# Where VectorE does the conformer's convolution steps of the first token half: one block behind the second value convolution, or spread between the token mixes

## The chip, the cores and the metric

One core of a Trainium2 chip runs the whole program. The time is the device time of one execution in microseconds (us); of several executions the median is given. TensorE (PE in the profile) multiplies matrices into PSUM, VectorE (DVE) and ScalarE (ACT) work on PSUM and SBUF, GpSimd (POOL) on SBUF, SyncE (SP) issues the copies from HBM.

## The reference, cut to what matters

Two transformer blocks follow each other. The first begins with four token mixers side by side (gMLP, gated delta rule, RWKV-7, a conformer convolution), each on 256 channels of 1024 tokens. Two pieces of it meet in this change:

```python
def conformer_conv(z, conv_w, conv_b, ln_g, ln_b):          # CONF_CONV = 31 taps
    z1, z2 = jnp.split(z, 2, axis=-1)
    h = z1 * jax.nn.sigmoid(z2)
    h = causal_depthwise_conv(h, conv_w) + conv_b
    h = layer_norm(h, ln_g, ln_b, LN_EPS)
    return jax.nn.silu(h)

# in rwkv7_time_mix
    P_prev = jnp.pad(P, ((0, 0), (1, 0), (0, 0)))[:, :-1]
    P = P + (P_prev - P) * mu
```

## The kernel before, in words

Channels lie on the 128 partitions and tokens along the free dimension. The first mixers work through the tokens in two halves of 512 (h = 0 and 1); 256 channels are two tiles (i = 0 and 1) of 128 x 512. Each engine runs a hand-written list of calls, strictly in order, and waits on semaphores where it needs another engine.

TensorE's list is made of units (L407): a unit multiplies 256 columns of w_in with the normalised tokens of one half, 32 matmuls into two PSUM tiles, and carries the name of what it makes (k, v, q, cs, cz, dg, r, rk, rv, rx, gu, gv). Between them stand the small products: transposes (L449), Gram matrices (L508), the block solves (L543 to L617) and so on. The weights of a unit are fetched by SyncE into one of two slots, as soon as TensorE has ended the unit two before (L795).

PSUM has 8 banks, and `Tiles.open` hands them out in turn: the n-th tile opened takes bank n modulo 8, and TensorE waits there until the engine that read the tile eight before has "taken" it. In the stretch that matters the tiles opened are, in order, gx 0, gx 1 (made for `spread_out`, L1500), then tok v 0, v 1, kk 0, kk 1, a 0, a 1 (taken by ScalarE, L1057 to L1061), then tok k 0 and k 1, which need the banks of gx 0 and gx 1, and after those the Gram tiles LT, AK, RB, RK (L508), which need the banks of v, kk, a and k.

On VectorE:

- `glu(0)` multiplies the two parts of the conformer's input. `taps_of(0)` is a generator of 62 steps, 31 taps by two channel tiles. Each step but the first two is one instruction (L1480) that multiplies the shifted 128 x 512 input by a weight per channel and adds it to the output; a step needs the step two before it, that of the same tile. `some(taps, n)` issues the next n steps.
- `mix(name, j, h)` (L1281, L1284) finishes a token mix behind ScalarE's L946, which first scales the unit's PSUM tile; one such pair for each tile i.
- `dn_scalars`, `values`, `q_scale`, `dn_decays` (L1295 to L1334) are small steps of the delta rule; `dn_grams` (L1342) masks its Gram tiles, beside GpSimd's L1674; `inverse` (L1369 to L1395) inverts triangular blocks.
- `conv("v", 1)` (L1254, L1269) is the short convolution of the second half's values; `spread_out(0)` (L1500, L1506) takes gx 0 and gx 1; `rw_grams(0)` (L1351 to L1357) masks RWKV's Gram tiles.

The result of the 62 steps is first read in `layer("cf", 0)`, far behind this stretch, and GpSimd copies the last 30 input columns of the half into the margin of the next when all 62 are done (L1703).

Of the kernel before, what the change touches and what calls it, by code (L numbers as in the profile page):

```python
# [30 lines left out]
class Env:  # L31
# [8 lines left out]
    def col(self, name, k=0):  # L40
        j = self.cols_at[name] + k
        return self.cols[:, j:j + 1]
# [271 lines left out]
def mixers_of_first_block(env):  # L314
# [21 lines left out]
    lt, rb, rk = (by_chunk(env.words(t, 0, 2 * T)) for t in (24, 26, 28))  # L336
# [43 lines left out]
    with stage(env, *names) as (block, *sems):  # L380
# [847 lines left out]
        def _(dve):  # L1228
# [46 lines left out]
            def mix(name, j, h, tiles_of=range(2)):  # L1275
                for i in tiles_of:
                    n = 2 * j + i
                    m, mu = rw[("r", "k", "v", "xwag")[j]][i], col("rw_mu", n)
                    dve.wait_ge(s["m_ready"], 8 * h + n + 1)
                    ps = tiles.ps(name, h, i)  # L1280
                    ins = v.scalar_tensor_tensor(m[:, 1:], ps[:, 0:HALF - 1], mu, m[:, 1:], ALU.mult, ALU.add)  # L1281
                    if h == 0:
                        ins.then_inc(s["mixed"], 1)
                        tiles.take(v.tensor_copy(hist_rw[:, n:n + 1], ps[:, HALF - 1:HALF]), name, h, i)  # L1284
                    else:
                        tiles.take(ins, name, h, i)
                        v.scalar_tensor_tensor(m[:, 0:1], hist_rw[:, n:n + 1], mu, m[:, 0:1], ALU.mult, ALU.add
                                               ).then_inc(s["mixed"], 1)
# [4 lines left out]
            def dn_scalars(h):  # L1293
                tiles.wait_taken(dve, "abt", h)
                dn_step(h, 1, v.tensor_tensor(chunks8(small["y"]), chunks8(small["ab"]), cols_of("dn_sgn", 8).unsqueeze(1).broadcast_to([P, CHUNKS, 8]), ALU.mult))  # L1295
                dn_step(h, 2, v.tensor_tensor(small["y"], small["y"], cols_of("dn_off", 32), ALU.add))
                if h == 0:
                    dve.wait_ge(s["rate_ready"], 1)
                dve.wait_ge(s["dn_act"], 8 * h + 3)
                dn_step(h, 3, v.scalar_tensor_tensor(small["sp"], small["y"], 0.0, small["l"], ALU.max, ALU.add))  # L1300
                sp = small["sp"].rearrange("p (c m) -> p c m", m=8)
                dn_step(h, 4, v.scalar_tensor_tensor(per_head(small["a16"]), sp[:, :, HEADS:8], -1.0, per_head(small["rate"]),
                                                     ALU.mult, ALU.mult))
                for j in range(2):
                    tiles.wait_taken(dve, "kt", h, j)
                sqk = env.words(O0, 0, 2 * T).rearrange("p (k two t) -> p k two t", k=2, two=2)[:, :, h, :]
                dn_step(h, 5, v.tensor_tensor(sqk, two(env.tile(4)), two(env.tile(4)), ALU.mult))
                dn_step(h, 6, v.tensor_reduce(small["ssq"].rearrange("p (k e) -> p k e", k=2),
                                              sqk.rearrange("p k (e d) -> p k e d", d=HD), AX_X, ALU.add))
                dve.wait_ge(s["dn_act"], 8 * h + 4)  # L1310
                dn_step(h, 7, v.scalar_tensor_tensor(per_head(small["lnc"]), sp[:, :, 0:HEADS], -1.0, per_head(small["lnq"]),
                                                     ALU.mult, ALU.subtract))

            def values(h):
                dve.wait_ge(s["dn_act"], 8 * h + 5)
                for j in range(2):
                    tiles.wait_taken(dve, "vt", h, j)
                x = env.words(2, 0, 2 * T).rearrange("p (n d) -> p n d", d=P)[:, :, 0:HD]
                v.tensor_tensor(x, x, small["vsc"].unsqueeze(2).broadcast_to([P, 16, HD]), ALU.mult).then_inc(s["r_values"], 1)

            def q_scale(h):
                for i in range(2):
                    dve.wait_ge(s["qn_ready"], 2 * h + i + 1)
                    v.scalar_tensor_tensor(q[i], q[i], HD ** -0.5, temp_g[1][i], ALU.mult, ALU.mult).then_inc(s["q_ready"], 1)

            def dn_decays(h):
                tiles.wait_taken(dve, "g", h)
                g, last = small["gsb"][:, 0:16], small["gsb"][:, 16:32]
                dn_step(h, 8, v.tensor_tensor(small["bias"], small["lnc"], g, ALU.subtract))
                dn_step(h, 9, v.tensor_tensor(small["kx"], small["bias"], last, ALU.add))  # L1330
                for e in range(2):
                    rows = slice(e * HD, (e + 1) * HD)
                    src = last[rows].rearrange("p (c i e) -> p c i e", i=2, e=2)[:, :, :, e]
                    dn_step(h, 10 + e, v.tensor_copy(small["dec2"][rows].rearrange("p (c i) -> p c i", i=2), src))  # L1334

            def dn_grams(h):
                for j in (0, 2):
                    for name, dst in (("KK", lt), ("QK", rb)):
                        for g in (j, j + 1):
                            dve.wait_ge(s["decay_step"], 8 * h + 4 + g + 1)  # L1340
                            tiles.wait(dve, name, h, g)
                            tiles.take(v.tensor_tensor(part(dst, g), quad(tiles.ps(name, h, g)), quad(exps[g % 2]), ALU.mult), name, h, g)  # L1342
# [127 lines left out]
            def taps_of(h):  # L1470
                w = lambda tap, i: col("cf_conv_w", 2 * tap + i)
                for back in range(TAPS_CF):
                    for i in range(2):
                        o, x = out_half(6 + i, h), cfh[:, i, TAPS_CF - 1 - back:TAPS_CF - 1 - back + HALF]
                        if back == 0:
                            dve.wait_ge(s["glu_ready"], 2 * h + i + 1)
                            ins = v.tensor_scalar(o, x, w(TAPS_CF - 1, i), col("cf_conv_b", i), ALU.mult, ALU.add)
                        else:
                            dve.wait_ge(s["cf_step"], 62 * h + 2 * back + i - 1)
                            ins = v.scalar_tensor_tensor(o, x, w(TAPS_CF - 1 - back, i), o, ALU.mult, ALU.add)  # L1480
                        ins.then_inc(s["cf_step"], 1)
                        yield

            def some(taps, n):
                for _ in range(n):
                    next(taps, None)
# [9 lines left out]
            def spread_out(h):  # L1496
                for i in range(2):
                    t = gm_v[i].rearrange("p (c t) -> p c t", t=P)
                    tiles.wait(dve, "gx", h, i)
                    ins = v.tensor_tensor(t, by_chunk(tiles.ps("gx", h, i)), b_s[:, i, :].unsqueeze(1).broadcast_to([P, CHUNKS, P]),  # L1500
                                          ALU.add)
                    tiles.take(ins, "gx", h, i)
                for i in range(2):
                    tiles.wait_taken(dve, "gx", h, i)
                    tiles.wait_taken(dve, "gu", h, i)
                    v.tensor_tensor(out_half(i, h), out_half(i, h), gm_v[i], ALU.mult)  # L1506
# [59 lines left out]
            conv("q", 0)  # L1566
            glu(0)
            taps = taps_of(0)
            some(taps, 12)
            dn_scalars(0)  # L1570
            mix("r", 0, 0)
            values(0)
            q_scale(0)
            some(taps, 4)
            mix("rk", 1, 0)
            dn_decays(0)
            some(taps, 6)
            mix("rv", 2, 0)
            some(taps, 14)
            mix("rx", 3, 0)  # L1580
            some(taps, 2)
            dn_grams(0)
            some(inverse("dn", 0), BLOCK)
            layer("gm", 0)
# [6 lines left out]
            dn_final(0)  # L1591
            decayed(0)
            conv("v", 1)
            some(taps, 62)
            spread_out(0)
            rw_grams(0)
            steps = inverse("rw", 0)
# [8 lines left out]
            taps = taps_of(1)  # L1606
# [3646 lines left out]
```

## Time and profile before

| | |
|---|---|
| median of 3 runs | 3183.69 us (3182.38 to 3184.23) |
| the profiled execution's own time | 3183.69 us |
| its span, from the first to the last instruction | 3181.4 us |
| busy share of the span | PE 97%, DVE 62%, POOL 42%, ACT 27% |

The profile shows for every instruction when it began and how long it took. A pause is printed in square brackets in front of the instruction that ended it, with its length and the instruction that released it. PEclk is the share of TensorE's full clock that was granted: 1.00 is 2.4 GHz, 0.50 is 1.2 GHz.

### The profile page before, as it was taken

Reading aid. Unit: us, or ns where it says so; the run is one execution under the profiler, and the core shown is the slowest. Engines: PE = TensorE matmul, PEld = TensorE weight load, DVE = VectorE, ACT = ScalarE, POOL = GpSimd, SP = SyncE. Lnnn points to the kernel's source line nnn. Section 1 sums busy time; section 2 is a strip of 40 time slices with the busy share of each in tenths; the row PEclk is TensorE's granted clock in tenths of the full one; section 3 lists DMA queues with packets and bytes.
Section 4 is the critical chain, followed back from the end, with each engine's and each line's share of the span. In section 5 each row is a group of like instructions: output and inputs, shape, how many; then the busy total and the mean of one; then the engine's idle time right before and its main releaser. Section 6 shows DMA issues by size and latency. Waiting matters only on the chain.

```text
span 3181.4 us, 35229 instructions
## 1 busy us (share of the span) xinstructions
PE 3073.9 (97%) x13146; PEld 2078.0 (65%) x13146; DVE 1984.8 (62%) x2716; ACT 861.0 (27%) x1530; POOL 1345.7 (42%) x1016
## 2 busy tenths in 40 slices
PE   8998998999999999999999999999999999999997
PEld 3445563874578888788644544544555588888886
DVE  2386888653578788787526654753125665577876
ACT  3343334321233333100213335203223344410002
POOL 0010010002599999555411000351015798855555
PEclk9999999999999999999999999999999999999998
DMA  4211111152222222666212111212121233376652
GB/s 142 67 60 34 50 34 53 54 172 93 80 80 85 85 100 90 226 234 227 67 54 90 57 54 53 77 43 66 53 80 53 113 140 146 126 254 234 220 197 81
DMA packets 206279, 335.70 MB, mean 106 GB/s; under 512 B 10145, under 2 KB 123297, under 8 KB 205345
## 3 DMA queue, kind: packets, MB, share of 16 engines
q1 hardware_dynamic: 204688, 330.45, 29.9%
q10 hardware_dynamic: 1424, 3.02, 0.3%
q8 instruction: 107, 1.75, 0.2%
q14 instruction: 60, 0.48, 0.0%
HBM read 269.21 MB, written 64.23 MB: 105 GB/s over the span
## 4 chain that ended last, share of the span: by engine, by line
PE 82%; DVE 9%; POOL 4%; ACT 2%; issue 1%; DMA 1%; ACTq 0%; SPq 0%; DVEq 0%; POOLq 0%
PE psum L3627 21%; PE psum L3907 14%; PE psum L181 10%; PE psum L2680 8%; PE psum L407 7%; PE psum L2082 3%; PE psum L4474 3%; PE psum L3644 2%; PE psum L563 1%; DVE arena L1380 1%; DVE arena L1378 1%; PE psum L4451 1%; PE psum L4412 1%; PE psum L2088 1%; DVE arena L1480 1%
## 5 line engine op out<-in xcount | busy, mean ns | idle before, releaser
L3627 PE MATMUL psum<-arena 128*128 128x256 f32 x2632 | 598.0, 381 | 14.2 <-DVE arena L3672 7.4
L3907 PE MATMUL psum<-arena 128*128 128x256 f32 x2660 | 585.9, 383 | 10.2 <-POOL arena L3933 5.3
L3907 PEld LDWEIGHTS psum<-arena 128*128 128x128 f32 x2660 | 510.7, 192 | 84.0 <-POOL arena L3933 7.1
L3627 PEld LDWEIGHTS psum<-arena 128*128 128x128 f32 x2632 | 499.4, 191 | 93.6 <-DVE arena L3672 11.2
L407 PE MATMUL psum<-arena 128*128 128x512 f32 x768 | 337.6, 598 | 7.1 <-DVE arena L1236 4.9
L181 PE MATMUL psum<-arena 128*128 128x512 f32 x768 | 332.4, 592 | 1.5 <-ACT arena L4644 1.5
L407 PEld LDWEIGHTS psum<-arena 128*128 128x128 f32 x768 | 146.0, 192 | 189.5 <-issue 184.8
L181 PEld LDWEIGHTS psum<-arena 128*128 128x128 f32 x768 | 145.8, 190 | 182.1 <-issue 180.6
L2680 PE MATMUL psum<-arena 128*128 128x512 f32 x576 | 251.5, 595 | 0.0
L2680 PEld LDWEIGHTS psum<-arena 128*128 128x128 f32 x576 | 109.0, 191 | 136.4 <-issue 136.4
L2369 DVE TENSOR_TENSOR arena<-arena 128x1024 f32<-128x1024 f32 x77 | 144.3, 1874 | 33.6 <-ACT arena L3664 23.8
L3930 POOL TENSOR_TENSOR arena<-arena 128x512 f32<-128x512 f32 (+1 forms) x49 | 74.9, 1529 | 208.6 <-PE psum L3907 78.6
L3627 PE MATMUL psum<-arena,consts_sb 128*128 128x256 f32 x632 | 155.7, 379 | 3.7 <-POOL consts_sb L3719 3.2
L3504 POOL TENSOR_TENSOR arena<-small_sb,consts_sb 128x512 f32<-128x512 f32 x16 | 16.2, 1041 | 324.3 <-PE psum L2760 169.5
L4871 DVE TENSOR_TENSOR arena<-arena 128x1024 f32<-128x1024 f32 x88 | 145.5, 1653 | 12.8 <-ACT arena L3655 8.3
L3664 ACT ACTIVATE conformer<-psum 128x256 f32<-128x256 f32 x238 | 90.6, 382 | 200.6 <-PE psum L3627 196.6
L4991 POOL TENSOR_TENSOR arena<-arena 128x512 f32<-128x512 f32 x75 | 98.5, 1314 | 102.4 <-DVE arena L4748 71.1
L2518 POOL TENSOR_TENSOR arena<-arena 128x512 f32<-128x512 f32 x42 | 57.4, 1366 | 181.0 <-ACT arena L2215 180.0
L3627 PEld LDWEIGHTS psum<-arena,consts_sb 128*128 128x128 f32 x632 | 119.7, 190 | 20.8 <-POOL consts_sb L3719 3.6
L3672 DVE TENSOR_TENSOR arena<-psum,conformer 128x256 f32<-128x256 f32 x238 | 98.6, 417 | 51.0 <-PE psum L3627 46.8
L2082 PE MATMUL psum<-arena 128*128 128x512 f32 x256 | 112.5, 592 | 0.0
L4474 PE MATMUL psum<-arena 128*128 128x512 f32 x224 | 97.0, 593 | 0.9 <-DVEq L241 0.9
(540 smaller groups left out, 4830.7 us busy)
## 6 DMA issues: line engine op xcount, KB each, us to landing
arena<-w_in SPq DMA_DIRECT2D x42, 1024.0 KB, 5.3
arena<-mlp_w SPq DMA_DIRECT2D x72, 512.0 KB, 6.9
arena<-w_ffn_down SPq DMA_DIRECT2D x36, 512.0 KB, 6.8
arena<-mlp_w SPq DMA_DIRECT2D x8, 2048.0 KB, 8.6
mlp_hidden_T<-arena SPq DMA_DIRECT2D x32, 512.0 KB, 2.6
arena<-mlp_hidden_T SPq DMA_DIRECT2D x16, 1024.0 KB, 5.6
arena<-w_out SPq DMA_DIRECT2D x12, 1024.0 KB, 5.4
mlp_hidden_B<-arena SPq DMA_DIRECT2D x24, 512.0 KB, 2.6
```

The source lines that it names most:

```text
L181: mm = nc.tensor.matmul(self.out(i, x.shape[1]), part, x, start=(kk == 0), stop=(kk == self.kt - 1))
L407: mm = nc.tensor.matmul(ps, slot(u)[:, k, m * P:(m + 1) * P], hn(k, h), start=(k == 0), stop=(k == KD - 1))
L2082: mm = nc.tensor.matmul(ps, plain_raw(v)[:, k, m * P:(m + 1) * P], half_of(env, N0, k, h), start=(k == 0), stop=(k == KD - 1))
L2369: hidden.mark(v_.tensor_tensor(to, one, two, ALU.add), name, q)
L2680: mm = nc.tensor.matmul(ps, slot(n)[:, k, m * P:(m + 1) * P], x_half(k, h), start=(k == 0), stop=(k == KD - 1))
L3627: mm = self.env.nc.tensor.matmul(self.ps(n, m), left[:, k, :], right[:, k, :], start=(m in (1, 5, 2) and k == 0), stop=(k == 1), skip_grou ...
L3664: self.copied.mark(self.env.nc.scalar.activation(to, self.ps(n, m), ACT.Copy), name, n)
L3672: self.blocks.mark(self.env.nc.vector.tensor_tensor(self.to(n, i, j), self.ps(n, m), self.temps[t][n % 2], ALU.add), name, n)
L3907: mm = self.env.nc.tensor.matmul(ps[:, 256 * r:256 * r + 256], left[:, s, r * P:(r + 1) * P], right[:, s, :], start=(first and s == 0 and ...
L4474: mm = nc.tensor.matmul(ps, left, mix_right[m](k), start=(k == 0), stop=(k == 3))
L4871: blocks.mark(v_.tensor_tensor(to, one, two, op), name, q)
L4991: fin(pool, nc.gpsimd.tensor_tensor(dst, dst, src, ALU.add), sem, value)
```

## The change

Before, the 62 steps of the first half were issued as 12, 4, 6, 14 and 2 between the calls in front of `dn_grams(0)`, and the other 24 in one block behind `conv("v", 1)`. After, all 62 are issued in front of the last mix, as 25, 3, 3, 4, 8, 11 and 8. For that, three calls of `mix` are split into one call for each channel tile, with steps between the two. No instruction is added, removed or altered; only VectorE's list has another order.

```diff
             taps = taps_of(0)
-            some(taps, 12)
+            some(taps, 25)
             dn_scalars(0)
-            mix("r", 0, 0)
+            mix("r", 0, 0, (0,))
+            some(taps, 3)
+            mix("r", 0, 0, (1,))
             values(0)
+            some(taps, 3)
             q_scale(0)
             some(taps, 4)
-            mix("rk", 1, 0)
+            mix("rk", 1, 0, (0,))
+            some(taps, 8)
+            mix("rk", 1, 0, (1,))
             dn_decays(0)
-            some(taps, 6)
-            mix("rv", 2, 0)
-            some(taps, 14)
+            some(taps, 11)
+            mix("rv", 2, 0, (0,))
+            some(taps, 8)
+            mix("rv", 2, 0, (1,))
             mix("rx", 3, 0)
-            some(taps, 2)
             dn_grams(0)
...
             conv("v", 1)
-            some(taps, 62)
             spread_out(0)
             rw_grams(0)
```

## Rows read from the trace of the kernel before

**Rows 1.** Page: share of the chain that ended last, by engine.
```profile
PE 82%; DVE 9%; POOL 4%; ACT 2%; issue 1%; DMA 1%; ACTq 0%; SPq 0%; DVEq 0%; POOLq 0%
```

**Rows 2.** Chain that ended last, 296 to 345 us: start, duration, what.
```profile
303.61 14.65 DVE arena L1480 x23
...
319.50 0.61 DVE arena L1500
...
320.25 1.94 PE psum L449 x8
```

**Rows 3.** Timeline of PE, 300 to 335 us: start, duration, instructions merged, pause before.
```profile
300.02 3.02 PE L449 MATMUL psum<-consts_sb,arena 128*128 128x128 f32 x24
320.25 1.94 PE L449 MATMUL psum<-consts_sb,arena 128*128 128x128 f32 x8 [17.22 <-DVE arena L1500]
322.13 4.63 PE L508 MATMUL psum<-arena 64*128 64x128 f32 x64
...
328.62 3.84 PE L508 MATMUL psum<-arena 64*128 64x128 f32 x64
...
334.23 13.95 PE L407 MATMUL psum<-arena 128*128 128x512 f32 x32
```

**Rows 4.** Timeline of DVE, 303 to 321 us.
```profile
303.52 15.98 DVE L1480 SCALAR_TENSOR_TENSOR arena<-conformer,cols_sb,arena 128x512 f32<-128x512 f32 x24
319.43 1.28 DVE L1500 TENSOR_TENSOR arena<-psum,arena 128x512 f32<-128x512 f32 x2
```

**Rows 5.** Windows: busy by engine, then PEclk, DMA share, GB/s.
```profile
303.00:320.00 17.00, 0.04 (x1) 0.00 (x0) 16.93 (x28) 4.18 (x8) 0.23 (x1) 0.61 0.01 2
320.00:323.00 3.00, 2.75 (x16) 2.45 (x18) 1.91 (x4) 1.19 (x2) 0.00 (x0) 0.50 0.00 0
...
348.00:396.00 48.00, 47.70 (x155) 23.45 (x155) 41.65 (x86) 17.68 (x30) 0.00 (x0) 1.00 0.24 70
```

**Rows 6.** Timeline of DVE, 98 to 179 us.
```profile
115.70 0.19 DVE L1295 TENSOR_TENSOR small_sb<-small_sb,cols_sb 128x32 f32<-128x32 f32 x1 [9.65 <-ACT small_sb L875]
...
129.19 0.75 DVE L1281 SCALAR_TENSOR_TENSOR arena<-psum,cols_sb,arena 128x511 f32<-128x511 f32 x1 [3.01 <-ACT arena L946]
...
134.69 1.29 DVE L1324 SCALAR_TENSOR_TENSOR arena<-arena 128x512 f32<-128x512 f32 x2 [3.19 <-ACT arena L928]
...
145.52 0.75 DVE L1281 SCALAR_TENSOR_TENSOR arena<-psum,cols_sb,arena 128x511 f32<-128x511 f32 x1 [6.05 <-ACT arena L946]
...
154.83 0.75 DVE L1281 SCALAR_TENSOR_TENSOR arena<-psum,cols_sb,arena 128x511 f32<-128x511 f32 x1 [3.71 <-ACT arena L946]
...
161.70 0.75 DVE L1281 SCALAR_TENSOR_TENSOR arena<-psum,cols_sb,arena 128x511 f32<-128x511 f32 x1 [6.05 <-ACT arena L946]
...
162.43 9.36 DVE L1480 SCALAR_TENSOR_TENSOR arena<-conformer,cols_sb,arena 128x512 f32<-128x512 f32 x14
...
175.43 0.75 DVE L1281 SCALAR_TENSOR_TENSOR arena<-psum,cols_sb,arena 128x511 f32<-128x511 f32 x1 [2.92 <-ACT arena L946]
...
176.16 2.44 DVE L1480 SCALAR_TENSOR_TENSOR arena<-conformer,cols_sb,arena 128x512 f32<-128x512 f32 x2
178.53 0.68 DVE L1342 TENSOR_TENSOR arena<-psum,arena 128x512 f32<-128x512 f32 x1
```

**Rows 7.** Timeline of POOL, 116 to 180 us: all its work there.
```profile
120.18 5.08 POOL L1668 TENSOR_TENSOR arena<-small_sb,consts_sb 128x512 f32<-128x512 f32 x4 [62.92 <-DVE small_sb L1302]
176.79 2.95 POOL L1674 TENSOR_TENSOR arena<-arena,consts_sb 128x512 f32<-128x512 f32 x2 [51.53 <-ACT arena L973]
```

**Rows 8.** Timeline of ACT, 306 us: the last copies before the pause.
```profile
306.08 1.11 ACT L1059 ACTIVATE arena<-psum 128x512 f32<-128x512 f32 x2
```

**Rows 9.** Timeline of PE: units (32 matmuls) behind two shorter pauses.
```profile
503.48 15.70 PE L407 MATMUL psum<-arena 128*128 128x512 f32 x32 [2.18 <-DVE arena L1281]
...
2282.74 13.97 PE L4451 MATMUL psum<-arena 128*128 128x512 f32 x32 [1.21 <-ACT arena L4665]
```

**Rows 10.** Page, DMA issues: count, KB each, us to landing.
```profile
arena<-w_in SPq DMA_DIRECT2D x42, 1024.0 KB, 5.3
```

## The prediction

> **What bounds the kernel now.** I read the page first. The chain that ended last lies on TensorE for 82% of the span and on VectorE for 9% [rows 1], so VectorE work is worth something only where it is in that chain. The change moves instructions of L1480, so next I asked the chain for the stretch behind `conv("v", 1)`. The steps stand in it: 23 of them in one piece from 303.61, then L1500, then TensorE's L449 at 320.25 [rows 2]. Then I read the two engines there. TensorE ends the transposes of v, kk and a at 300.02 + 3.02 = 303.04, and then pauses 17.22 us until VectorE's L1500 releases it [rows 3]. VectorE meanwhile does 24 steps in 15.98 us, from 303.52, and starts L1500 at 319.43 [rows 4]. The reader should see why the one waits for the other. The tiles of tok k need the banks of gx, gx is taken by `spread_out`, and `spread_out` stands behind the 24 steps, which nothing needs yet. This is an order in a list, not a lack of VectorE time.
>
> The windows add something that the chain does not say. TensorE's mean clock in the 17 us of the pause is 0.61, and in the 3 us behind it 0.50, which is 1.2 GHz [rows 5]. So the pause is paid twice: once as idle time and once as slow matmuls behind it.
>
> Last I looked at where the steps go. Between 98 and 179 us VectorE has seven pauses that matter: 9.65, 3.01, 3.19, 6.05, 3.71, 6.05 and 2.92 us, 34.6 us together, each ended by ScalarE [rows 6].
>
> **What the change removes.** The 24 steps leave the path: L1500 can start at 303.52 instead of 319.43 [rows 4], which is 15.91 us. What it needs is there: gx was made by matmuls in front of the transposes that TensorE started at 300.02 [rows 3].
>
> The second part is the clock. After the change TensorE pauses from 303.04 until L1500 has taken gx 0. Before, it went on 0.82 us after L1500 had started (320.25 against 319.43), so now that is at 303.52 + 0.82 = 304.34: a pause of 1.3 us. No row shows this very pause, so I bound its effect from both sides. If the clock falls nevertheless, as behind the pause of 2.18 us, whose unit took 15.70 us [rows 9] against the 13.95 of an undisturbed one [rows 3], nothing more is gained. If it stays up, the eight L449 take a third of the 3.02 us of the 24 before them, 1.01 instead of 1.94, and the 64 L508 the 3.84 of their second group instead of 4.63 [rows 3]: 0.93 + 0.79 = 1.72 us. A unit behind a pause of 1.21 us took 13.97 [rows 9], as an undisturbed one; 1.3 is nearest to that row, so I take the clock as kept.
>
> Not all of the 1.72 can be had, because other engines then set the pace. The second tile of tok k must wait for the second L1500 (half of 1.28 us later). And ScalarE, whose list is in order, ends its copies of kk and a at 306.08 + 1.11 = 307.19 [rows 8]. It can take tok k only then, two copies of the same size, until about 308.3, and the tiles of RK need those two banks. RK is the last quarter of the 64 L508, some 0.96 us, so it ends at about 309.4. With a cold clock it would end at 322.13 + 4.63 - 15.91 = 310.85. That is 1.4 us; I take 1.3 for the semaphores between.
>
> Sum: 15.9 + 1.3 = 17.2 us.
>
> **What it adds in front.** The 24 steps now lie in the pauses. One step costs 9.36 / 14 = 0.67 us [rows 6], and 15.98 / 24 gives the same [rows 4]. The first pause begins at 115.70 - 9.65 = 106.05; 13 more steps are 8.7 us against 9.65. Then 3 are 2.0 against 3.01, 3 are 2.0 against 3.19, and 8 are 5.3 against 6.05. Before the first rv mix 5 more are 3.3 against 3.71, and before the second 8 are 5.3 against 6.05 [rows 6]. Every group fits, with 0.35 us to spare at the tightest. So each mix and each small step starts when it did, and ScalarE and TensorE see no difference; cost 0. The four steps in front of the rk mix stay where they were. The cover is thin, but if a group runs over, the mixes behind it only come late, and the list has slack again: the last 2.92 us pause stays, and 14 + 2 steps that stood around the rx mix are gone, 9.36 + 2.44 us [rows 6].
>
> The two steps that go from 176.16 took 2.44 us, 1.22 each, beside GpSimd's L1674 [rows 6, 7]. The first Gram mask there could start 178.53 - 176.16 = 2.4 us sooner, but the one behind it waits for GpSimd, and TensorE has no use for it: I count nothing. In the new places GpSimd is idle except from 120.18 to 125.26 [rows 7], when VectorE does `dn_scalars` as before. GpSimd's margin copy waits for step 62 and comes sooner; it is 0.23 us of the window in which it stands [rows 5] and nothing waits closely for it. No copy from HBM is issued by what moves.
>
> **What is late next.** Behind 304 TensorE has no pause to give the gain back in: from 348 to 396 it is busy 47.70 of 48 us, VectorE 41.65 [rows 5], and both start from the L508 that have moved. The weights move along, since a unit's copy is issued when the unit two before has ended. A copy lands in 5.3 us [rows 10] and has a whole unit, 13.95 us [rows 3], to do so.
>
> So the span is 3181.4 - 17.2 = 3164.2 us. The profiled execution took 3183.69 us, 2.3 around its span, and equals the median of the runs; so the forecast is 3183.69 - 17.2 = 3166.5 us.
>
> **The rivals.**
>
> First, the clock falls all the same. For it speaks that 2.18 us were enough once [rows 9], and that TensorE will have small waits behind the 1.3 us pause too, at the second gx and at tok k. Then only the 15.9 us come: 3167.8 us. The Trainium skill, "TensorE: Matmul & The Clock Gate", section "A second HAM failure mode: psum-queue depth-cycling", says that a PE that idles briefly again and again while it goes round the PSUM banks can swing between the two clock levels. By that rule this rival would be the likelier one; the unit behind 1.21 us at full speed [rows 9] speaks against it, and no row here has several short waits in the same few us. I give it 0.24.
>
> Second, the steps do not fit, and the change only moves the delay. If none of the pauses could be used (each pause's releaser then comes as much later), 24 x 0.67 = 16.0 us would arrive at `dn_grams` and from there at TensorE: 17.2 - 16.0 = 1.2 us faster, 3182.5. Against it: the pauses end with ScalarE, which waits for TensorE's units and not for VectorE, so they are real. 0.03.
>
> Third, the gain is given back at a wait that does not move, say a unit whose weights come late. The price is at most 17.2 us, so the time lies up to 3183.7; it begins where a copy takes longer than the 13.95 us of a unit, against 5.3 [rows 3, 10]. 0.03.
>
> Fourth, the other side: the steps are slower in the new places, as the two beside GpSimd. The 62 steps have the time that 38 took before, 36 x 0.67 + 2.44 = 26.4 us, and the 34.6 us of pauses, 61.0 together. With 17.2 us of gain on top they may take 78.2, 1.26 each, before the kernel is slower; at 1.40 each they take 86.8, which makes 8.6 us more, 3192.3. Even the pace beside GpSimd, 1.22, stays below, and GpSimd works in only 5.08 of these 78 us [rows 7]. The Trainium skill, "GPSIMD Engine Reference", section "8. Key points", says that GpSimd shares its SBUF interfaces with VectorE and that instructions with two SBUF inputs, which these steps are, contend with it. No run here shows which other engine could do the same. 0.02.
>
> **How the numbers follow.** The forecast holds 0.68, the rivals 0.24, 0.03, 0.03 and 0.02. The predicted time is the forecast's, 3166.5. The clock's bounds give 3183.7 - 15.9 - 1.7 = 3166.1 to 3167.8. The three runs lie 1.3 below and 0.5 above their median, which makes 3164.8 to 3168.3. A later short pause, like that of 2.18 us, can lose or keep its clock when what comes before has moved: 15.70 - 13.95 = 1.75 us, taken as 1.8 upwards and 1.0 downwards. So the range is 3163.8 to 3170.1. 0.2%, 6.4 us, is about what a measurement of this kernel can tell from no change. Faster by more holds the forecast, the first rival and half of the third, 0.68 + 0.24 + 0.015, about 0.94; within it the second and the rest of the third, 0.04; slower the fourth, 0.02.
>
> **What would show it.** In the profile after: no L1480 between 300 and 320 us; L1500 at about 303.5; TensorE's pause in front of the last eight L449 about 1.3 us instead of 17.2; PEclk 1.00 from 304 to 310; the unit that starts at 334.23 now at about 317.0; the pauses of rows 6 down to 0.3 to 1.2 us with the instructions behind them at the same times. The prediction is wrong if a mix or `dn_scalars` starts later than before by more than a few tenths, if TensorE shows a pause between 98 and 300 us that it did not have, or if the difference of 17 us at that unit is smaller at 400 us or at the end.

## The result, and the profile after

The changed kernel takes 3166.89 us in the median of six runs (3163.02 to 3169.91), the kernel before 3183.96 (3182.38 to 3184.63): a ratio of 0.9946, 95% interval 0.9936 to 0.9957, so 0.54% faster. The forecast was 3166.5 us in a range of 3163.8 to 3170.1.

I read the profile after in the order of the forecast's own list. First the timeline of PE in the stretch behind `conv("v", 1)`, which answers to [rows 3]:

```profile
299.59 3.02 PE L449 MATMUL psum<-consts_sb,arena 128*128 128x128 f32 x24
303.92 1.16 PE L449 MATMUL psum<-consts_sb,arena 128*128 128x128 f32 x8 [1.32 <-DVE arena L1500]
305.01 4.03 PE L508 MATMUL psum<-arena 64*128 64x128 f32 x64
...
310.91 3.84 PE L508 MATMUL psum<-arena 64*128 64x128 f32 x64
...
316.51 13.95 PE L407 MATMUL psum<-arena 128*128 128x512 f32 x32
```

The pause in front of the last eight L449 is 1.32 us instead of 17.22. All of this profile lies 0.43 us earlier than that of before (the 24 L449 at 299.59, not 300.02). The difference is there from the first unit on (19.25 us against 19.68), far in front of anything that the change touches, so here and below I measure from the start of those 24 to the start of the next unit, L407: 334.23 - 300.02 = 34.21 us before, 316.51 - 299.59 = 16.92 after. That is 17.29 us less.

On DVE, [rows 4] become one line. The steps are gone, and L1500 follows the last instructions of `conv("v", 1)` directly:

```profile
301.81 1.37 DVE L1269 SCALAR_TENSOR_TENSOR arena<-small_sb,cols_sb,arena 128x1 f32<-128x1 f32 x6
303.09 1.28 DVE L1500 TENSOR_TENSOR arena<-psum,arena 128x512 f32<-128x512 f32 x2
```

The windows, which answer to [rows 5]. PEclk is the third number from the right:

```profile
303.00:306.00 3.00, 2.08 (x24) 1.82 (x26) 2.58 (x5) 2.98 (x7) 0.00 (x0) 1.00 0.00 0
306.00:310.00 4.00, 4.00 (x61) 3.88 (x58) 2.90 (x5) 2.72 (x6) 0.00 (x0) 1.00 0.00 0
...
331.00:379.00 48.00, 47.66 (x157) 23.25 (x155) 41.71 (x85) 17.86 (x30) 0.00 (x0) 1.00 0.25 76
```

TensorE's clock stays at 1.00 through the pause and behind it, where it was 0.61 and 0.50. In the 48 us behind the next unit, from 331 to 379 us (348 to 396 before), TensorE is as busy as before, 47.66 of 48 us.

In front, the timeline of DVE that answers to [rows 6]:

```profile
115.27 0.19 DVE L1295 TENSOR_TENSOR small_sb<-small_sb,cols_sb 128x32 f32<-128x32 f32 x1 [1.04 <-ACT small_sb L875]
...
128.76 0.75 DVE L1281 SCALAR_TENSOR_TENSOR arena<-psum,cols_sb,arena 128x511 f32<-128x511 f32 x1 [1.02 <-ACT arena L946]
...
134.26 1.29 DVE L1324 SCALAR_TENSOR_TENSOR arena<-arena 128x512 f32<-128x512 f32 x2 [1.21 <-ACT arena L928]
...
145.09 0.75 DVE L1281 SCALAR_TENSOR_TENSOR arena<-psum,cols_sb,arena 128x511 f32<-128x511 f32 x1 [0.76 <-ACT arena L946]
...
154.40 0.75 DVE L1281 SCALAR_TENSOR_TENSOR arena<-psum,cols_sb,arena 128x511 f32<-128x511 f32 x1 [0.39 <-ACT arena L946]
...
161.26 0.75 DVE L1281 SCALAR_TENSOR_TENSOR arena<-psum,cols_sb,arena 128x511 f32<-128x511 f32 x1 [0.75 <-ACT arena L946]
...
175.00 0.75 DVE L1281 SCALAR_TENSOR_TENSOR arena<-psum,cols_sb,arena 128x511 f32<-128x511 f32 x1 [6.05 <-ACT arena L946]
...
177.67 0.69 DVE L1342 TENSOR_TENSOR arena<-psum,arena 128x512 f32<-128x512 f32 x1 [1.85 <-POOL arena L1678]
```

The pauses have shrunk to 1.04, 1.02, 1.21, 0.76, 0.39 and 0.75 us, and the instruction behind each starts where it did, less the 0.43 us of the whole profile (115.27 for 115.70, 161.26 for 161.70). Nothing is late.

The first block solve of RWKV starts 17.7 us sooner than before (L543, 392.60 for 410.27), and the span is 18.1 us shorter: 0.43 in front of the change, 17.29 in the stretch, the remaining 0.4 in later stages. Only the 17.29 us are shown to come from the change.

### The profile page after: what moved, and what is told of

Its sections match the earlier page's. It is cut to its first block, busy times and chain, and to the rows that moved or that the text cites. A ratio compares the mean times of both kernels' runs of the same rounds, so it can differ in the third digit from the quotient of the medians.

```text
span 3163.3 us, 35229 instructions
## 1 busy us (share of the span) xinstructions
PE 3067.8 (97%) x13146; PEld 2073.4 (66%) x13146; DVE 1983.9 (63%) x2716; ACT 862.1 (27%) x1530; POOL 1345.1 (43%) x1016
## 3 DMA queue, kind: packets, MB, share of 16 engines
q8 instruction: 107, 1.75, 0.2%
## 4 chain that ended last, share of the span: by engine, by line
PE 82%; DVE 9%; POOL 4%; ACT 2%; issue 1%; DMA 1%; ACTq 0%; SPq 0%; DVEq 0%; POOLq 0%
PE psum L3631 21%; PE psum L3911 13%; PE psum L181 10%; PE psum L2684 8%; PE psum L407 7%; PE psum L2086 3%; PE psum L4478 3%; PE psum L3648 2%; PE psum L563 1%; DVE arena L1380 1%; DVE arena L1378 1%; PE psum L4455 1%; PE psum L4416 1%; PE psum L2092 1%; DVE arena L1391 1%
## 5 line engine op out<-in xcount | busy, mean ns | idle before, releaser
L407 PE MATMUL psum<-arena 128*128 128x512 f32 x768 | 337.6, 598 | 7.2 <-DVE arena L1236 4.9
L407 PEld LDWEIGHTS psum<-arena 128*128 128x128 f32 x768 | 146.0, 192 | 189.5 <-issue 184.7
L4875 DVE TENSOR_TENSOR arena<-arena 128x1024 f32<-128x1024 f32 x88 | 149.0, 1693 | 12.6 <-ACT arena L3659 8.1
```

Source lines behind the costliest of these rows:

```text
L407: mm = nc.tensor.matmul(ps, slot(u)[:, k, m * P:(m + 1) * P], hn(k, h), start=(k == 0), stop=(k == KD - 1))
L4875: blocks.mark(v_.tensor_tensor(to, one, two, op), name, q)
```

## The experiments

Times are medians; the kernel before ran on the same chip beside each group: 3184.39 us beside lump_late, lump_early, warm and behind_grams, 3183.54 beside keep3, keep8, second_half and after_again, 3185.12 beside warm16 and all_first. "Stretch" is the measure of above, from the 24 L449 to the next unit. In kernels with added or removed lines the line numbers behind them are shifted by up to 5.

| run | us | ratio to before, interval | TensorE's pause before L449 | stretch |
|---|---|---|---|---|
| after_again | 3166.95 | 0.9947, 0.9930 to 0.9963 | 1.32 | 16.92 |
| lump_early | 3166.48 | 0.9944, 0.9929 to 0.9959 | 1.32 | 16.91 |
| all_first | 3174.11 | 0.9967, 0.9954 to 0.9980 | 1.32 | 16.92 |
| lump_late | 3186.70 | 1.0007, 0.9998 to 1.0017 | 1.32 | 16.92 |
| behind_grams | 3184.04 | 0.9999, 0.9990 to 1.0009 | 1.32 | 16.92 |
| keep3 | 3170.19 | 0.9955, 0.9941 to 0.9970 | 3.30 | 20.22 |
| keep8 | 3174.32 | 0.9969, 0.9957 to 0.9981 | 6.62 | 23.80 |
| warm16 | 3183.61 | 0.9998, 0.9989 to 1.0008 | filled | 32.63 |
| warm | 3194.24 | 1.0031, 1.0018 to 1.0044 | filled | 44.70 |
| second_half | 3155.91 | 0.9912, 0.9897 to 0.9927 | 1.31 | 16.92 |

**Is the spreading needed, and how deep is the cover?** Three kernels are the one before with the 24 steps in another place (in all_first all 62 steps, so 50 are moved), and with no mix split.

```diff
# lump_early: in front of dn_scalars(0)
-            some(taps, 12)
+            some(taps, 36)
             dn_scalars(0)
...
-            some(taps, 62)
             spread_out(0)
```

> Before, with the 24 steps put in one block in front of dn_scalars(0) (36 instead of 12), no mix split. They run over ScalarE's release there (9.65 us of pause for 16 us of steps), so dn_scalars starts some 6.4 us later. Theory (TensorE needs those small results only about 20 us later, and VectorE catches up in its later pauses): the time of the change, 3165 to 3169, the same 1.3 us pause before L1500, no new pause of TensorE between 98 and 300. Rival (the spreading itself is needed): a new TensorE pause between 120 and 180 us and up to 6.4 us lost, 3170 to 3174.

The timeline of DVE:

```profile
99.62 22.61 DVE L1480 SCALAR_TENSOR_TENSOR arena<-conformer,cols_sb,arena 128x512 f32<-128x512 f32 x34
122.15 0.18 DVE L1295 TENSOR_TENSOR small_sb<-small_sb,cols_sb 128x32 f32<-128x32 f32 x1
...
145.81 0.75 DVE L1281 SCALAR_TENSOR_TENSOR arena<-psum,cols_sb,arena 128x511 f32<-128x511 f32 x1 [3.33 <-ACT arena L946]
...
175.72 0.75 DVE L1281 SCALAR_TENSOR_TENSOR arena<-psum,cols_sb,arena 128x511 f32<-128x511 f32 x1 [2.92 <-ACT arena L946]
```

`dn_scalars` starts at 122.15 instead of 115.70 [rows 6], and VectorE has no pause there at all. The delay is eaten by 145.81, where a pause of 3.33 us is left of 6.05, and at 175.72 the pause is the old 2.92. TensorE has no new pause, and the stretch is 16.91 us. So the theory holds: one block in one place brings the whole gain, and the splits of the mixes bring nothing on top.

```diff
# all_first: everything in front of dn_scalars(0)
-            some(taps, 12)
+            some(taps, 62)
             dn_scalars(0)
```

> Before, with all 62 steps in one block in front of dn_scalars(0), 50 more than there and none later. dn_scalars starts at about 140 instead of 115.7, 25 us late. Theory (the cover in front of dn_scalars is about 20 us, then ScalarE's list stalls behind the small results and with it the banks that TensorE waits for): a new TensorE pause of 2 to 10 us between 128 and 180 us, 3168 to 3177. Rival (VectorE's list has any amount of slack in front of dn_grams): 3166 to 3167.5, no new pause.

The timeline of PE, then a line of DVE, and last the line of PE in the change that the 32 L487 are compared with:

```profile
149.38 0.58 PE L480 MATMUL psum<-small_sb,consts_sb 128*128 128x16 f32 x2 [4.96 <-DVE small_sb L1284]
...
150.32 3.68 PE L487 MATMUL psum<-consts_sb,small_sb 128*64 128x128 f32 x32
```

```profile
142.97 0.18 DVE L1302 SCALAR_TENSOR_TENSOR small_sb<-small_sb 128x16 f32<-128x16 f32 x1
```

```profile
144.61 1.97 PE L487 MATMUL psum<-consts_sb,small_sb 128*64 128x128 f32 x32
```

Here the cover ends, as the theory had it. TensorE waits 4.96 us at L480. L480 multiplies a result of `dn_scalars`, but that (L1302) was done at 143.15, before the pause began at 149.38 - 4.96 = 144.42. What the pause waits for is L1284, with which VectorE ends the mix of r and frees its bank: the tile that L480 writes is the eighth opened behind r's first tile, so it needs that bank. The mix is late because it follows ScalarE, whose list had stopped behind the late small results. Behind the pause TensorE's clock is 0.50 (149.4 to 154 us), and L487 takes 3.68 us instead of 1.97. From L480 to the end of the two units behind L487 it is 33.13 us (149.38 to 182.51) against 29.92 in the change (144.16 to 174.08), 3.2 more, so 4.96 + 3.2 = 8.2 us are lost in all. The time is 0.33% under that of before, where the change's is 0.54% under.

```diff
# lump_late: in front of dn_grams(0)
-            some(taps, 2)
+            some(taps, 26)
             dn_grams(0)
...
-            some(taps, 62)
             spread_out(0)
```

> Before, with the 24 steps taken from behind the second value convolution and put in one block in front of dn_grams(0). Theory (the gain is VectorE time taken from TensorE's path, and it is kept only where the steps fill real waits): dn_grams(0) starts 24 x 0.67 = 16 us later, at about 194.5, TensorE gets a pause of 11 to 16 us between 200 and 245 us, its wait for L1500 is still only about 1.3 us, and the time is 3178 to 3185 us, at most 5 us under before. Rival (it only matters that the block leaves the front of L1500): the delay at dn_grams is absorbed, and the time is that of the change, 3166 to 3168.

The timeline of PE:

```profile
179.99 1.16 PE L508 MATMUL psum<-arena 64*128 64x128 f32 x16
196.63 2.08 PE L508 MATMUL psum<-arena 64*128 64x128 f32 x16 [15.48 <-DVE arena L1342]
198.64 14.98 PE L407 MATMUL psum<-arena 128*128 128x512 f32 x32
...
334.36 13.95 PE L407 MATMUL psum<-arena 128*128 128x512 f32 x32
```

The pause has only moved: 15.48 us at the Gram matrices, behind VectorE's L1342, and the slow matmuls behind it moved with it (16 L508 in 2.08 us where the 16 in front take 1.16; the unit 14.98 where an undisturbed one has 13.95 [rows 3]). Nothing is gained; the next unit of the stretch starts at 334.36, as before (334.23). The theory had the pause's size, but not its place (200 to 245 us: it comes already between the Gram matrices themselves), and the time lies above its range of 3178 to 3185. So what the steps are moved in front of decides, not that they leave L1500.

**Is TensorE's release enough?** The same 24 steps, one call later:

```diff
# behind_grams
             conv("v", 1)
-            some(taps, 62)
             spread_out(0)
             rw_grams(0)
+            some(taps, 62)
             steps = inverse("rw", 0)
```

> Before, with the 24 steps moved behind rw_grams(0), in front of the inverse: TensorE is released as in the change, but VectorE's chain is not relieved. Theory (in the stretch behind, VectorE's chain is nearly as tight as TensorE's): TensorE's pause before the last eight L449 is 1.3 us, its unit starts about 17 us sooner than before, but then it waits 10 to 13 us at the rates of the second half (L480 to L487), where it had nearly no pause; 3177 to 3181 us, a gain of 3 to 7. Rival (only the release of TensorE matters): 3166 to 3168.

The timeline of PE:

```profile
305.47 1.16 PE L449 MATMUL psum<-consts_sb,arena 128*128 128x128 f32 x8 [1.32 <-DVE arena L1500]
...
318.06 13.95 PE L407 MATMUL psum<-arena 128*128 128x512 f32 x32
...
359.53 1.12 PE L449 MATMUL psum<-consts_sb,arena 128*128 128x128 f32 x4 [11.58 <-DVE arena L1254]
360.44 15.03 PE L407 MATMUL psum<-arena 128*128 128x512 f32 x32
...
395.16 1.09 PE L487 MATMUL psum<-consts_sb,small_sb 128*64 128x128 f32 x16 [2.87 <-ACT arena L856]
```

The release is the same, 1.32 us and a stretch of 16.92. Then the gain is given back, 11.58 us at L449, which waits for VectorE's L1254, and 2.87 at L487. My theory had the mechanism but not the place: I looked at the small results of the second half, but the first to run dry is the bank that `conv("q", 1)` holds, a call in the middle of the inverse. Nor is 3 to 7 us left over: the ratio is 0.9999. VectorE's chain behind L1500 has no room for 16 us.

**What is the clock's part?** First the pause of before, filled with useless matmuls in a bank that is free then:

```diff
# warm: range(32); warm16: range(16); in front of the transposes of tok k, h = 0
+                        tiles.wait_taken(pe, "tok", "v", 0, 0)
+                        for _ in range(16):
+                            nc.tensor.matmul(tiles.ps("tok", "v", 0, 0), const["ident"], hn(0, 0), start=True, stop=True)
```

> Before, with 32 useless 128x512 matmuls that TensorE does in its pause of 17 us, into a bank that is free then. Theory (part of the pause's cost is the low clock behind it): PEclk 1.00 from 310 to 327, the eight L449 take about 1.0 instead of 1.94 us and the 64 L508 about 3.9 instead of 4.63, and the unit that starts at 334.23 before starts 1.3 to 1.7 us sooner; time 3182 to 3183. Rival (these are slow because of banks or of ScalarE): the same 1.94 and 4.63 us, no difference.

One call is two matmul instructions in the profile, so the 32 calls lasted 27.7 us and became the limit themselves; the time says nothing. Behind them the eight L449 took 1.04 us and the 64 L508 3.84. The run with half as many:

> As the run with useless matmuls in TensorE's pause, but half as many of them (32 matmul instructions of 128x512, about 13.9 us), so that they end before L1500 starts and do not become the limit themselves. Theory: PEclk 1.00 behind the pause, the eight L449 about 1.04 to 1.2 us, the 64 L508 about 3.84 to 4.0; the unit behind starts 1.3 to 1.7 us sooner than in before, 3182 to 3183 us where before is 3184. Rival (the low clock costs nothing that others do not take): no difference in the unit's start.

The timeline of PE, and the window that answers to the first of [rows 5]:

```profile
299.27 3.01 PE L449 MATMUL psum<-consts_sb,arena 128*128 128x128 f32 x24
304.14 13.97 PE L659 MATMUL psum<-arena,consts_sb 128*128 128x512 f32 x32 [1.86 <-ACT arena L1065]
319.41 1.25 PE L449 MATMUL psum<-consts_sb,arena 128*128 128x128 f32 x8 [1.29 <-DVE arena L1504]
320.59 3.84 PE L508 MATMUL psum<-arena 64*128 64x128 f32 x64
...
331.90 13.95 PE L407 MATMUL psum<-arena 128*128 128x512 f32 x32
```

```profile
303.00:320.00 17.00, 14.56 (x36) 6.42 (x36) 17.00 (x27) 3.44 (x7) 0.23 (x1) 1.00 0.00 0
```

TensorE still waits for L1500, but comes out of it with its full clock: 1.25 and 3.84 us instead of 1.94 and 4.63. The stretch is 32.63 us, 1.58 under before. That is the price of the low clock in the kernel before, shown with the wait itself left in. The whole time, 3183.61 against 3185.12, has an interval that includes no change.

Then the change with some of the 24 steps left behind `conv("v", 1)`:

```diff
# keep3 (keep8 in brackets): from the group in front of the second rv mix
-            some(taps, 8)
+            some(taps, 5)      # (0)
             mix("rv", 2, 0, (1,))
...
             conv("v", 1)
+            some(taps, 62)
             spread_out(0)
```

> The change, but with 3 of the 24 steps left behind the second value convolution. TensorE's pause before the last eight L449 becomes 1.3 + 2.0 = 3.3 us. If the clock stays up behind it, the unit behind starts 2.0 us later than in the change, 3168.9 against 3166.9; if it falls as behind the pause of 17 us, 3.4 to 3.7 us later, about 3170.4.

> The change, but with 8 of the 24 steps left behind the second value convolution. TensorE's pause becomes 1.3 + 5.3 = 6.6 us and the clock falls in it: the unit behind starts 5.3 + 1.4 = 6.7 us later than in the change, 3173.6. If steps count by their own length alone, 5.3 us later, 3172.2.

The timelines of PE, keep3 first, with its window behind the pause:

```profile
300.26 3.01 PE L449 MATMUL psum<-consts_sb,arena 128*128 128x128 f32 x24
306.58 1.64 PE L449 MATMUL psum<-consts_sb,arena 128*128 128x128 f32 x8 [3.30 <-DVE arena L1500]
308.15 4.86 PE L508 MATMUL psum<-arena 64*128 64x128 f32 x64
...
320.48 10.09 PE L407 MATMUL psum<-arena 128*128 128x512 f32 x23
```

```profile
306.50:310.00 3.50, 3.42 (x24) 3.01 (x26) 1.73 (x3) 2.13 (x4) 0.00 (x0) 0.56 0.00 0
```

```profile
299.95 3.01 PE L449 MATMUL psum<-consts_sb,arena 128*128 128x128 f32 x24
309.57 1.94 PE L449 MATMUL psum<-consts_sb,arena 128*128 128x128 f32 x8 [6.62 <-DVE arena L1500]
311.44 4.84 PE L508 MATMUL psum<-arena 64*128 64x128 f32 x64
...
323.75 6.66 PE L407 MATMUL psum<-arena 128*128 128x512 f32 x15
```

Three steps are 2.0 us, but the stretch is 20.22 - 16.92 = 3.30 us longer. Eight are 5.3, and it is 6.88 longer. The extra 1.3 and 1.6 us are the clock: 0.56 behind the pause of 3.30 us, 0.50 behind that of 6.62 (309.5 to 313 us), and L508 at 4.86 and 4.84 where the change has 4.03. Both times are near the values expected with a fallen clock (3170.19 us for 3170.4, 3174.32 for 3173.6). Behind the 1.32 us of the change it is 1.00. So the last three steps that leave the path are worth more than their own length, 3.3 us for 2.0.

**Does the rule hold elsewhere?** Behind this stretch stands a pause of the same kind. TensorE waits 7.64 us for L1480, for the last steps of the second half. Nine of these go into VectorE's waits around `solve` and `carry`:

```diff
# second_half: the change, and
-            some(taps, 20)
+            some(taps, 21)
             solve("rw", 0)
+            some(taps, 4)
             carry("rw", 0)
-            some(taps, 24)
+            some(taps, 28)
```

> The change, and in the second half 9 of the 18 late steps moved into VectorE's waits around solve and carry of RWKV's first half (1 in front of solve, 4 between solve and carry, 4 behind carry; pauses of 0.8, 3.3 and 2.9 us there). Theory (the same rule holds: a step in a real wait costs nothing, a step in front of what TensorE waits for costs its length): TensorE's pause of 7.64 us before the centre of the conformer's second layer norm shrinks to about 1.6, its eight L672 take about 3.6 instead of 5.1, and the time is 6.0 to 7.5 us less than the change's, 3159.5 to 3161. Rival (VectorE's chain there waits for something else that now comes late): less than 2 us.

The timeline of PE in the change, and then in this run:

```profile
503.42 7.03 PE L407 MATMUL psum<-arena 128*128 128x512 f32 x16
518.09 5.14 PE L672 MATMUL psum<-arena,consts_sb 128*128 128x512 f32 x8 [7.64 <-DVE arena L1480]
...
538.36 12.46 PE L563 MATMUL psum<-arena 128*128 128x128 f32 x96 [2.37 <-ACT arena L1078]
```

```profile
502.79 7.03 PE L407 MATMUL psum<-arena 128*128 128x512 f32 x16
509.92 3.70 PE L672 MATMUL psum<-arena,consts_sb 128*128 128x512 f32 x8
...
528.74 10.96 PE L563 MATMUL psum<-arena 128*128 128x128 f32 x96 [2.35 <-ACT arena L1078]
```

3155.91 us, 11.0 under the change of the same group and 0.88% under before: the fastest of all. The direction was right and my size too small. From the 24 L449 to the L672, it is 518.09 - 299.59 = 218.50 us in the change and 509.92 - 299.03 = 210.89 here, 7.6 less: nine steps are 6.05, and I had overlooked that the mix of rv between the two groups of nine, 1.57 us in VectorE's list, also stands in front of the last step. Then the clock: L672 takes 3.70 us instead of 5.14, and the 96 L563, which took 12.46 in the change, 10.96. Together 7.6 + 1.4 + 1.5 = 10.5; up to L571, which follows the L563, it is 10.6. The 1.5 us were not in the expectation. The pause in front of L563 is the same in both runs (2.37 and 2.35 us), but behind it the clock is 0.50 in the change (538.3 to 541 us) and 1.00 here (528.7 to 531). In the other ten profiles the 96 L563 take 12.4 to 12.6 us, all of them with the long pause at L672 still in front. Why the same pause lets the clock fall there and not here stays open.

**Is the gain the same in every execution?**

> The changed kernel again, unaltered. Its six runs lie between 3163.0 and 3169.9, three times as far apart as those of before. If the stretch up to 400 us is the same to 0.2 us in this profile, the spread comes from later stages, and the gain of the moved steps is 17.3 us in every execution.

The stretch is 16.92 us again, and L543 starts 93.00 us behind the 24 L449, 93.01 in the first profile. So the stretch is the same in both profiled executions, and it is 16.91 to 16.92 us in lump_early, all_first, lump_late, behind_grams and second_half too. Where the spread of the runs comes from is not shown: the two profiled executions took 3165.57 and 3166.21 us and lie too close together to tell. Nor is the spread peculiar to the change. With more runs the kernel before spreads as far, 3179.03 to 3186.27 us in the fourteen beside warm16.

## Why the prediction was right

- The path. TensorE waited for a bank, the bank for `spread_out`, and `spread_out` for 24 steps that nobody needed yet. The chain that ended last now goes through these lines without L1480:

```profile
303.09 0.70 DVE arena L1500
...
303.92 1.16 PE psum L449 x8
```

- The 15.9 us. TensorE resumes 0.83 us behind the start of L1500, as before (0.82). Of the 17.29 us of the stretch, 17.22 - 1.32 = 15.90 are the pause.
- The clock. I took 1.3 us of at most 1.72; it is 17.29 - 15.90 = 1.39. The eight L449 need 1.16 us, not 1.01, because the second gx comes late, and the first 64 L508 4.03, not 3.84, because ScalarE takes tok k only then: these were the two limits of that step. The first rival, that the clock falls all the same, did not occur: PEclk is 1.00 from 303 to 310 us. The Trainium skill, "TensorE: Matmul & The Clock Gate", section "A second HAM failure mode: psum-queue depth-cycling", tells of a kernel whose clock swings because TensorE often idles for a moment between groups of matmuls as it goes round the banks. Here it did not swing, but the test is weak: behind the pause the waits add up to about 0.3 us (1.16 - 1.04 and 4.03 - 3.84). The clock did fall behind the 3.30 us of keep3.
- The cover in front. Every group fitted, with 0.39 us left where I had 0.35. But the step was stricter than it had to be: lump_early shows that the pauses need not be met one by one, since TensorE needs what `dn_scalars` and the mixes make only much later. all_first shows where that ends.
- The second rival, that the steps only move the delay, was false for the places that were chosen and true for one block in front of `dn_grams`, only some 15 us behind the last of them. Its price, 16.0 us, was right up to the clock: lump_late has 15.48 us of pause and no gain at all, where I had left 1.2.
- The fourth rival did not occur: a step takes 15.33 / 23 = 0.67 us in the new place. But the prediction read its row wrongly. The two steps beside L1674 did not take 1.22 us each: the first, which began in front of L1674, took 0.74 and the second 1.79. So a step beside GpSimd is slower than the 1.26 that the prediction allowed; what saved the sum is that GpSimd works so little there.
- What is late next. TensorE and VectorE both moved by the same 17 us, so nothing was given back. behind_grams shows that this was no matter of course: had only TensorE moved, all would have been lost 40 us later. So of the prediction's two reasons the first, that TensorE has no pause there to give the gain back in, does not carry: it holds for behind_grams as well. What counts is the second, that VectorE starts from the same moved L508.
- The range. The 1.8 us that I allowed for the later pause of 2.2 us is not real. In the first profile the unit behind it takes 15.70 us; in after_again it takes 14.00, and then TensorE waits 1.78 us for L1494:

```profile
487.11 14.00 PE L407 MATMUL psum<-arena 128*128 128x512 f32 x32 [2.20 <-DVE arena L1281]
502.89 1.95 PE L455 MATMUL psum<-arena,consts_sb 128*128 128x512 f32 x4 [1.78 <-DVE arena L1494]
```

Either way the next unit starts 17.6 us behind this one (485.86 to 503.42, 487.11 to 504.68). The median falls in the middle of the range, but the single runs (3163.02 to 3169.91) fill nearly all of it and one lies below, so that a median of few runs fell this close to 3166.5 is in part luck; the 17.29 us of the stretch are not.

## What to carry to other kernels

Ask of each instruction in an in-order list who needs its result and when, and move what is needed late out of the way of what another engine waits for, to a place where the delay dies out before its results are needed; it need not fill single pauses to the microsecond. Check the list behind the wait as well: releasing one engine brings nothing if the releasing engine's own chain is the next limit. And where TensorE waits, count the slow matmuls behind the pause too, and remove the last few microseconds of it: here the last 2.0 us of steps cost 3.3.

## What had not been expected

- In front of the last eight L449 the low clock has a price of its own of 1.3 to 1.6 us, measured in three ways: 1.39 us in the change, 1.58 with the pause filled, 1.3 and 1.6 beyond the length of three and eight steps. It is not the same behind every pause. Behind the 4.96 us of all_first it is 3.2 us, and behind the same 7.64 us at L672 the eight matmuls take 5.09 to 6.73 us in eleven profiles, against 3.70 in second_half, where the pause is gone: 1.4 to 3.0 us.
- The same pause of 2.2 us in front of a unit is followed by a slow unit (15.70 us) in six of the twelve profiles and by a fast one (14.00) in the other six. What decides it is not shown.
- Two steps beside GpSimd's L1674 took 2.44 us [rows 6], and L1674 itself 2.95 [rows 7]; without them GpSimd takes 2.50 for the same two. Both engines lose in this overlap, and VectorE's loss is all in the step that began beside L1674 (1.79 us, the other 0.74). In lump_late, where more steps follow, two steps beside it take 1.79 and 1.75 us, and the next 0.74 again.
